# Dense products between the real ones in attention and rotation, and two banks for a unit's output

## The reference

```python
# 8 MLA heads: q, k of 96 dimensions, the last 32 of them rotated by position
q = concat([q[..., :64], rope(q[..., 64:], pos)])
k = concat([k[..., :64], rope(k[..., 64:], pos)])
o_mla = block_causal_attention(q, k, v, 1 / sqrt(96), key_valid)
# 8 forget-gate heads of 64 dimensions, with a cumulative log gate: s += cum[t] - cum[s]
o_fox = block_causal_attention(fq, fk, fv, 1 / sqrt(64), key_valid, cum)
return concat([o_mla, o_fox]) @ w_out
# block_causal_attention, by blocks of 128 queries i, over the keys [0, (i + 1) * 128)
s = q_i @ k.T * scale;  s = where(mask, s, -1e30);  p = softmax(s);  o_i = p @ v
```

## Time and profile before

| | |
|---|---|
| median of 3 runs | 3329.11 us (3324.34 to 3329.39) |
| the profiled execution, its own time | 3333.59 us |
| its span in the trace | 3331.9 us |
| PE matmul busy | 2814.7 us, 84% of the span |
| rotation stage | 467.1 to 495.4 us |
| attention stage, first score to last mix | 495.4 to 608.9 us |
| output projection | 608.9 to 637.8 us |
| mean granted clock of PE over the span | 0.906 |

### The profile page before, as it was taken

One profiled execution on the slowest core, in us unless ns is written; L12 is line 12 of the kernel. 1 busy time (PEld: TensorE's weight loads), 2 busy tenths in 40 slices (PEclk: granted clock), 3 DMA queues, 4 the chain that ended last, 5 costly groups with the idle time before them and its releaser, 6 DMA issues. The chain is left out here.

```text
span 3331.9 us, 58393 instructions
## 1 busy us (share of the span) xinstructions
PE 2814.7 (84%) x25561; PEld 1970.7 (59%) x25561; DVE 1089.3 (33%) x2188; ACT 506.9 (15%) x1104; POOL 312.3 (9%) x342
## 2 busy tenths in 40 slices
PE   6998979899998988797877569889988976978775
PEld 5887835688886443543444334368888875544443
DVE  3563263254523331210100232166565522101012
ACT  1000112100010100100000110044444321000001
POOL 0000000000000000211111020032222201111110
PEclk8999765798989999798999889899999987989998
DMA  6785100376713211899999712000000017999994
GB/s 210 231 251 164 57 26 1 101 252 204 213 60 117 76 38 67 312 394 403 403 403 403 288 43 68 18 3 4 3 4 3 4 52 301 403 409 406 407 403 197
DMA packets 279700, 616.55 MB, mean 185 GB/s; under 512 B 28900, under 2 KB 182007, under 8 KB 245412
## 3 DMA queue, kind: packets, MB, share of 16 engines
q1 hardware_dynamic: 237584, 539.56, 43.9%
q10 hardware_dynamic: 30756, 59.18, 5.0%
q0 software_dynamic: 11120, 14.23, 1.3%
HBM read 612.76 MB, written 21.08 MB: 190 GB/s over the span
## 5 line engine op out<-in xcount | busy, mean ns | idle before, releaser
L1949 PE MATMUL bank<-expert_weights,ex_xt 128*64 128x256 f32 x2688 | 314.8, 390 | 97.9 <-DMA expert_weights<-in_moe_w_up_dram 75.4
L1949 PEld LDWEIGHTS bank<-expert_weights,ex_xt 128*64 128x64 f32 x2688 | 215.8, 141 | 211.6 <-issue 144.6
L449 PE MATMUL bank<-u,weights 128*128 128x272 f32 (+1 forms) x1408 | 319.5, 391 | 14.0 <-DVEq L472 14.0
L449 PEld LDWEIGHTS bank<-u,weights 128*128 128x128 f32 x1408 | 271.3, 193 | 62.2 <-DVEq L472 14.8
L1154 DVE SCALAR_TENSOR_TENSOR ada_acc<-ada_w,cond,ada_acc 128x512 f32 (+1 forms) x336 | 227.5, 744 | 1.6 <-PEq L421 1.6
L1860 DVE TENSOR_TENSOR ex_hidden<-ex_silu,bank 128x256 f32<-128x256 f32 x64 | 26.9, 421 | 599.1 <-ACT ex_silu L1998 575.5
L527 PE MATMUL bank<-rw_mixed,weights 128*128 128x512 f32 (+2 forms) x448 | 188.6, 582 | 31.7 <-DVEq L538 28.2
L1949 PE MATMUL bank<-weights,ex_xt 128*64 128x256 f32 x1408 | 164.2, 389 | 32.4 <-DMA weights<-in_moe_w_up_dram 31.0
L1970 PE MATMUL bank<-expert_weights,ex_hidden_turned 128*64 128x512 f32 x672 | 158.8, 616 | 21.7 <-DVE ex_hidden_turned L1863 21.7
L1949 PEld LDWEIGHTS bank<-weights,ex_xt 128*64 128x64 f32 x1408 | 110.4, 140 | 92.3 <-issue 53.3
L527 PEld LDWEIGHTS bank<-rw_mixed,weights 128*128 128x128 f32 (+1 forms) x448 | 83.9, 189 | 136.7 <-issue 134.9
(11 more groups left out here) (512 smaller groups left out, 4180.3 us busy)
## 6 DMA issues: line engine op xcount, KB each, us to landing
expert_weights<-in_moe_w_gate_dram SPq DMA_DIRECT2D x84, 1024.0 KB, 24.3
expert_weights<-in_moe_w_up_dram SPq DMA_DIRECT2D x84, 1024.0 KB
expert_weights<-in_moe_w_down_dram SPq DMA_DIRECT2D x84, 1024.0 KB, 25.0
ada_w<-in_ada_w_dram ACTq DMA_DIRECT2D x24, 2048.0 KB, 8.8
weights<-in_moe_w_gate_dram SPq DMA_DIRECT2D x44, 1024.0 KB
weights<-in_moe_w_up_dram SPq DMA_DIRECT2D x44, 1024.0 KB
weights<-in_moe_w_down_dram SPq DMA_DIRECT2D x44, 1024.0 KB
weights<-in_w_gate_dram SPq DMA_DIRECT2D x22, 1024.0 KB, 5.5
```

The lines of the kernel that those rows point to most:

```text
L449: last = nc.tensor.matmul(k.bank[b + side * NB][:, 0:N], w[:, f, c * P:(c + 1) * P], rhs[:, f, 0:N], start=(f == 5), stop=(f == 4))
L1949: last = nc.tensor.matmul(half_cols(k.bank[2 + side], t), xt[:, s, f * SLOTS:(f + 1) * SLOTS], w[:, q * 512 + t * 256:q * 512 + t * 256 + ...
```

## The change

In the rotation stage, every real product is followed by one product of `k.ones` (128 x 128) with a chunk of `k.x`'s context tokens, 256 columns that are read twice to make 512, into bank 7. In attention, the scores of each unit are followed by two such products, of chunks 0 and 2. Nobody reads bank 7 in these stages, and no instruction waits for these products or signals their end. To free bank 7 from the outputs of the units, these have banks 5 and 6 in turn instead of 5, 6 and 7. The wait before the mix of unit u is therefore for `kept` of unit u - 2, where it was u - 3.

```diff
--- rope_stage, PE
                 nc.tensor.matmul(k.bank[n % 4][0:QK, 0:TA], k.rope_turn[0:QK, 0:QK], x[0:QK, h, :],
                                  start=True, stop=True).then_inc(turned, 1)
+                nc.tensor.matmul(k.bank[7][:, :], k.ones[:, :], k.x[:, n % DC, SEQ:TB].unsqueeze(1).broadcast_to([P, 2, SEQ]),
+                                 start=True, stop=True)
--- attention_stage
+    WARM = 2
...
-                if u >= 3:
-                    pe.wait_ge(kept, u - 2)
+                if u >= 2:
+                    pe.wait_ge(kept, u - 1)
...
-                    last = nc.tensor.matmul(k.bank[5 + u % 3][r:r + RH, 0:P], vm[0:n, c, h * RH:(h + 1) * RH],
+                    last = nc.tensor.matmul(k.bank[5 + u % 2][r:r + RH, 0:P], vm[0:n, c, h * RH:(h + 1) * RH],
...
                 if u < U:
                     scores(u)
+                    for n in range(WARM):
+                        nc.tensor.matmul(k.bank[7][:, :], k.ones[:, :], k.x[:, 2 * n, SEQ:TB].unsqueeze(1).broadcast_to([P, 2, SEQ]),
+                                         start=True, stop=True)
...
-                    nc.scalar.activation(o[r:r + RH, h // 2, t * P:(t + 1) * P], k.bank[5 + v % 3][r:r + RH, 0:P],
+                    nc.scalar.activation(o[r:r + RH, h // 2, t * P:(t + 1) * P], k.bank[5 + v % 2][r:r + RH, 0:P],
```

## The result

The changed kernel takes 3333.41 us as the median of 20 executions (3326.77 to 3339.48), the kernel before 3327.75 us beside it (20 executions, 3322.72 to 3332.52). The ratio is 1.002, 95% interval 1.0013 to 1.0026: slower by 5.7 us, interval 4.3 to 8.7. That is 0.17%, under the 0.2% (6.7 us) that the prediction took as its bound, and 0.8 us from the forecast of +6.5 us.

The account below looks back on a forecast made before the run. PE at half clock was taken to bound attention. Terms 6.4 + 0.6 - 0.8 + 1.8 + 0 - 1.4 gave +6.6 us, taken as +6.5 on the 3329.11 us median: 3335.6 us, range 3330 to 3345.

Parts of the forecast that it names:

- Does the clock rise: Attention: dense 128-row blocks, 3.4 us at half clock in every unit, raise PE's clock and keep it up; nearly sure.
- The rival in which it stays down: Dense blocks do not raise the clock: attention +109 us, rotation +16, giving 3454 us; chance 0.06.
- What the real work is worth at full clock: Attention: streaming halves, gaps shrink by 0.78; with dense products MLA pairs +0.83 us, forget-gate pairs -0.03, together +6.4 us.
- Entries of the dense products: Attention: gaps for weight loads where dense products follow products of fewer rows; 0.6 us taken, for MLA units.
- Every dense instruction pays its load: Rival: 0.1 us weight load on each of attention's 128 dense instructions, 13 us, rotation perhaps 1; 3349 us; chance 0.05.
- The dense block covers the gaps: Faster rival: loads behind attention's dense blocks get ahead, removing 21.8 us of gaps; -15 us, 3314 us; chance 0.06.
- Cold start: Start of attention: after about 3 us of PE idling it begins at half clock; +1.8 us, at most 3.3.
- Fill: Start of attention: PE's 0.8 us wait before the first transposes disappears under dense work; -0.8 us.
- Two banks: Attention: mix waits for the output kept two units before, not three; slack 1.8 us, so cost 0.
- Drain: End of attention, no dense products: halving already counted in pairs; last transposes, copies and mixes lack under 0.5 us cover.
- Rotation: Rotation: dense products hidden by PE's lead over VectorE; cost 0, bound 2 us if the rise is late, 16 if absent.
- Output projection: Behind attention: begins at full clock instead of 2.87 us at half clock; -1.4 us, 0 at the least.

Follow-up runs that it names:

- experiment 3: Changed kernel with one dense product per attention unit instead of two; 3305.51 us, ratio 0.9944 to the kernel before.
- 8: Changed kernel with attention's dense products on 8 of the 128 rows of both operands; 3442.57 us in one execution.
- 12: Changed kernel with dense products ahead of the scores: two in units 0 to 3, 256 columns per forget-gate unit; two banks; 3321.63 us, ratio 0.9993.
- seventh: Changed kernel with four more dense products behind the rotation, none in MLA units, 256 columns per forget-gate unit; 3293.88 to 3300.08 or 3322.02 to 3345.45 us.
- tenth: Changed kernel with four dense products behind the rotation, three banks, 512 columns ahead of scores in every fourth MLA and every forget-gate unit; 3302.07 us.
- 9: Changed kernel with dense products ahead of the scores: two in units 0 to 3, 256 columns per forget-gate unit; three banks; 3313.65 us, ratio 0.9972.
- 4: Changed kernel with attention's dense products in units 0 to 3 alone; 3315.76 us, ratio 0.9968 to the kernel before.
- 6: Changed kernel with two dense products in units 0 to 3, then only 256 dense columns per forget-gate unit; 3297.78 us, 3293.3 us when repeated.
- 1: Changed kernel without attention's dense products, keeping the rotation's and the two banks; 3327.05 us, ratio 0.9999 to the kernel before.
- 5: Changed kernel with two dense products in units 0 to 3, then only one of 512 columns per forget-gate unit; 3305.56 us, ratio 0.9926.

## Why the prediction was right, point by point

- *What bounds attention:* right. PE is busy 121.1 of 122.4 us, and every dense instruction taken out came back as time (experiment 3).
- *Does the clock rise:* right, after the first 3.7 us. The rival in which it stays down was one change of shape away: with 8 rows it came true, at 3442.6 us against the 3454 worked out for it, of which 16 were for a rotation at half clock, where this kernel kept its products of 128 rows and ran at 0.92 (8).
- *What the real work is worth at full clock:* 8 MLA pairs by +0.80, in place of +0.83, and 8 forget-gate pairs by +0.10, in place of -0.03. The real parts are 6.74 - 3.42 = 3.32 us (forecast 3.35) and 8.21 - 3.42 = 4.79. Of the 4.79, 0.2 are the entries of the next point, and 4.59 stand against 4.66. The gaps have shrunk to (3.32 - 2.30) / 1.35 = 0.76 and (4.59 - 2.99) / 2.14 = 0.75, where I had 0.78. The rows behind it give 0.33 / 0.40 = 0.83; for going under that the prediction gave no reason, so that the factor came out near is luck. With 0.83 the sum had been 1.4 us higher.
- *Entries of the dense products:* the term was mis-sized, and sat in the wrong family. I had 0.6 us for MLA and none for the forget gate. MLA has none: 1.72 us for four instructions is 0.430 each. Each forget-gate unit has 0.10 (1.82 us), 1.6 in all. A dense block behind the 96-row scores costs only its streaming, one behind the gates' 2-row product 0.10 more, and one between a mix and the 64-row scores 0.20 more (12). The real parts came out 0.8 us under the forecast (8 x 0.03 + 8 x 0.07) and the entries 1.0 over it, so that the pairs' total, +7.2 against +7.0, is near in part because two errors cancel.
- *Every dense instruction pays its load* (the rival): refuted by the same 0.430. The Trainium skill ("TensorE: Matmul & The Clock Gate", "The mechanism") says, in its list of what overlaps, that a load overlaps running matmuls only when its row group differs; this trace disagrees for products of 128 rows.
- *The dense block covers the gaps* (the rival on the faster side): refuted. Taking half the block away left the real part as it was (6.74 - 5.02 = 1.72, all of it streaming).
- *Cold start:* 494.19 to 497.58 for four dense instructions, 3.7 us at half clock in all: +1.85, where I had +1.8. The seventh and tenth kernels show that the gap causes it, since without the gap it is gone.
- *Fill:* the 0.8 us wait for the probabilities is gone, as forecast.
- *Two banks:* 0 in the steady units, right: the slack of 1.8 us was the dense block itself, 1.7 us. Without it five of six MLA pairs wait, and the two banks cost 0.28 us in each (9 against 4, 6 and 12).
- *Drain:* the term was mis-sized. PE waits 0.6 us in it for `kept`, where I had looked for no such wait, and that is most of the 0.7 us by which fill and drain exceed the forecast (attention's 8.9 less 6.4, 0.8, 1.85, and plus 0.8). But it is not the price of the two banks. With three banks and full clock (10) PE is idle for 0.34 and 0.19 us before the same two mixes, and from the same transposes to the projection it takes 4.82 us (577.22 to 582.04) against 4.87. What binds is most likely the chain of copies behind the last transposes (the sixth kernel's trace names one, 0.34 us at 571.29), for which I had "under 0.5 us" and moved the sum by only 0.1, and that to the faster side.
- *Rotation:* 0, right (1). A product and its dense one take 1.32 us, 470.55 to 471.87, against VectorE's 1.30.
- *Output projection:* -1.42 (29.28 to 27.86), where I had -1.4: right. The 28.9 us before and the 27.6 after that I named are both 0.3 to 0.4 short, by the stretch of the earlier trace rows that ends too early.
- *Sum:* the stages give +8.9 + 0 - 1.4 = +7.5, where I had +6.5; the medians give +5.7 (4.3 to 8.7). The mechanism holds term by term, and the errors of a term are each under 2 us. That the total lies 0.8 us from the medians is closer than either can tell and in part luck. On which side of the bound of 0.2% the change would fall was left open: the forecast's own chances were 0.41 and 0.42, and with the rivals slower had the larger one (0.53).

The terms put together say more than their sum. The clock is worth 8 x (5.94 - 3.32) + 8 x (8.11 - 4.79) = 47.5 us here, and the 128 dense instructions cost 128 x 0.427 = 54.7. Break-even is near 111 of them (47.5 / 0.427). The other terms, +1.85 - 0.8 + 0.7 - 1.4, come to nearly nothing. The change is no gain because it pays for the clock in every unit, where the MLA units, once raised, hold it unpaid (4) and half the dense products are enough elsewhere (3).

## What to carry to other kernels

Products that nobody reads raised PE's clock here when they filled all 128 rows, and not on 8; on the engine that sets the end they cost what they stream. So work out what the clock is worth to the real instructions first (their gaps shrink to about 0.75, not to 0.5), and stay under that. Then raise the clock once, read from the trace in which stretch the real work loses it again, and put filler there alone; take several executions, since a kernel near the edge has two times. Filler also covers waits for buffers, so look at these again when you thin it out.

## What the runs showed of the hardware

- Products of 8 rows took longer than ones of 128 rows and the same columns, 0.93 against 0.85 us at half clock, with PE busy without a gap for 224 us at 0.50 (8, one execution).
- The MLA units, at 0.50 for their whole length before, held 1.00 for 12 units, some 23 us, once they had it (4, and again in 5 and 6). So the same instructions run at either level, depending on what stood before them.
- The same 256 columns per forget-gate unit went with 3290 to 3302 us in nine executions of nine behind the scores (6), with 3294 to 3300 in four of ten with the bridge and no dense product in the first units (7), and with 3310 to 3328 in all nineteen ahead of the scores, where both profiled ones lost the clock (9, 12). What tells them apart was not found.
